# Entry of the expert loop: where the second norm's sums, the slot lists and the routing of a mixture-of-experts layer are worked out

## The reference, cut to what matters

```python
x = x + g1 * (merged @ w_out[l])                                # output projection of the mixers
h = rmsnorm(x, norm_ffn_g[l]) * (1.0 + sc2) + sh2               # second norm
y = swiglu(h2, w_shared_gu[l], w_shared_down[l]) + moe_routed(h2, router_w[l], router_bias[l], w_exp_gu[l], w_exp_down[l])
x = x + g2 * y
# moe_routed: scores = sigmoid(h2 @ router_w); the 6 best of 64 experts by scores + bias;
#   gate = score / sum of the 6 scores * 2.5; every expert runs SwiGLU (1024 -> 256 -> 1024) on its tokens,
#   and each token adds its 6 results, each times its gate
```

## Time and profile before

| what | us |
|---|---|
| median of 3 runs (lowest, highest) | 3300.69 (3299.34, 3303.19) |
| the profiled execution, its own time | 3301.01 |
| its span, first to last instruction | 3299.4 |
| busy TensorE / VectorE / ScalarE / GpSimd | 2927.4 / 2033.5 / 1552.3 / 578.8 |
| mean granted clock of TensorE | 0.937 of full |
| DMA mean | 204 GB/s |

### The profile page before, as it was taken

One profiled execution on the slowest core, in us unless ns is written; L12 is line 12 of the kernel. 1 busy time (PEld: TensorE's weight loads), 2 busy tenths in 40 slices (PEclk: granted clock), 3 DMA queues, 4 the chain that ended last, 5 costly groups with the idle time before them and its releaser, 6 DMA issues. The chain is left out here.

```text
span 3299.4 us, 42492 instructions
## 1 busy us (share of the span) xinstructions
PE 2927.4 (89%) x13828; PEld 2230.6 (68%) x13828; DVE 2033.5 (62%) x2874; ACT 1552.3 (47%) x2406; POOL 578.8 (18%) x569
## 2 busy tenths in 40 slices
PE   2899998899879999999369999989997999999983
PEld 1577776677667777777256777756775777777762
DVE  3544446555568888888345444464546788888854
ACT  0342333432347777777023324243223677777740
POOL 0100000000143333333010000000003333333310
PEclk9899999999889999999669999999987999999985
DMA  8123332224369999997422243312334899999944
GB/s 206 60 90 114 122 121 97 80 103 139 121 255 362 369 369 368 357 364 294 159 64 71 95 141 108 128 58 91 130 126 170 301 369 352 371 366 366 360 149 178
DMA packets 119235, 671.95 MB, mean 204 GB/s; under 512 B 27372, under 2 KB 28652, under 8 KB 84364
## 3 DMA queue, kind: packets, MB, share of 16 engines
q1 hardware_dynamic: 86476, 608.19, 50.2%
q0 software_dynamic: 31456, 57.70, 5.3%
q10 hardware_dynamic: 1152, 4.19, 0.3%
HBM read 655.20 MB, written 56.98 MB: 216 GB/s over the span
## 5 line engine op out<-in xcount | busy, mean ns | idle before, releaser
L1790 DVE TENSOR_TENSOR ew_lo<-ew,e_hi 128x2048 fp32r<-128x2048 f32 x256 | 586.7, 2292 | 187.4 <-ACT e_hi L1649 187.3
L670 PE MATMUL bank<-h_hi,w_hi 128*128 128x512 f32 x1248 | 515.0, 413 | 39.2 <-DVE gt L753 14.3
L1649 ACT ACTIVATE e_hi<-ew 128x2048 fp32r<-128x2048 f32 x256 | 489.8, 1914 | 102.1 <-PE bank L1935 78.3
L604 DVE TENSOR_TENSOR w_lo<-raw,w_hi 128x1024 fp32r<-128x1024 f32 x198 | 242.7, 1226 | 426.7 <-ACT w_hi L596 426.5
L670 PE MATMUL bank<-h_hi,w_lo 128*128 128x512 f32 x1248 | 503.7, 404 | 0.0
L670 PE MATMUL bank<-h_lo,w_hi 128*128 128x512 f32 x1248 | 501.3, 402 | 0.0
L1935 PE MATMUL bank<-e_hi,x_hi 128*128 128x512 f32 x1024 | 413.2, 404 | 0.0
L1935 PE MATMUL bank<-ew_lo,x_hi 128*128 128x512 f32 x1024 | 402.3, 393 | 0.0
L1935 PE MATMUL bank<-e_hi,x_lo 128*128 128x512 f32 x1024 | 400.1, 391 | 0.0
L1558 POOL DMA_INDIRECT y_d<-y,idx x128 | 217.4, 1698 | 623.8 <-issue 526.3
L596 ACT ACTIVATE w_hi<-raw 128x1024 fp32r<-128x1024 f32 x198 | 208.3, 1052 | 250.4 <-DMA raw<-in_wmix 179.2
(11 more groups left out here) (293 smaller groups left out, 4474.3 us busy)
## 6 DMA issues: line engine op xcount, KB each, us to landing
ew<-in_wexp SPq DMA_DIRECT2D x128, 2048.0 KB, 9.6
raw<-in_wmix SPq DMA_DIRECT2D x294, 512.0 KB, 4.0
ew<-in_wexp SPq DMA_DIRECT2D x128, 1024.0 KB, 9.3
yt<-y_d SPq DMA_DIRECT2D x8, 3072.0 KB, 10.1
ada<-in_ada SPq DMA_DIRECT2D x4, 2048.0 KB, 18.0
ew<-in_wexp SPq DMA_DIRECT2D x2, 3072.0 KB, 10.4
h_d<-htok ACTq DMA_DIRECT2D x8, 512.0 KB, 2.9
v_d<-vB SPq DMA_DIRECT2D x1, 3840.0 KB
```

The source lines that it names most:

```text
L604: nc.vector.tensor_tensor(w_lo[q % SPLIT][:], raw[u % RAW][:], w_hi[q % SPLIT][:].bitcast(F32), ALU.subtract).then_inc(lo_done, 1)
L670: ins = nc.tensor.matmul(out, lhs, rhs, start=start, stop=stop)
L1649: nc.scalar.activation(e_hi[h][:], up_part(ew, j, h), ACT.Copy).then_inc(whi_done, 1)
L1790: nc.vector.tensor_tensor(up_part(ew_lo, j, h), up_part(ew, j, h), e_hi[h][:].bitcast(F32), ALU.subtract).then_inc(wlo_done, 1)
```

## The change: what it does

- **Norm sums.** They leave the block of the experts. Beside the output projection ScalarE squares block k of `xT` one job after it was made, and TensorE adds one matmul of 512 columns with a column of ones (float32, result 1 x 512). The new block starts with a copy of that row to `srow`, four matmuls that turn it into a column for each token block, the mean, the root and the spread as before.
- **Norm's application.** VectorE does all 8 `hf` first; ScalarE adds all 8 shifts, loads the sigmoid's table by an early dummy, makes 3 of the `h_hi`, the sigmoid, and the others between the copies to `htok`. The logits wait for `hf` only.
- **Routing beside the shared expert.** TensorE runs jobs 0 and 1 before the ranks and 2 and 3 behind them, then the slot lists, jobs 4 to 9, the turning of expert 0's tokens, jobs 10 and 11. VectorE's routing is laced with the splits and evacuations of those jobs.
- **Slot lists.** VectorE makes `at_slot` (a pair's rank against 0 to 127, 24 x 128 values a partition); GpSimd makes `filed` (one-hot times result row + 1, and one-hot times gate: two instructions of 1536 values a partition); 24 matmuls of 128 columns sum their products into a bank (slot x expert): result row + 1 and gate. VectorE makes `slots` from it, and the gathers start from there. The write to `slot_d` remains (overflow blocks read it), 3 indirect DMAs in each of the first 8 steps of GpSimd's loop. The filling of `xg` with zeros and the reading back are gone.
- **Result rows.** Row choice*512 + token instead of token*6 + choice; the last block's load therefore reads 6 pieces of 4 KB, 2 MB apart, for a token.
- **Early first split.** ScalarE and VectorE split the weights of expert 0 while TensorE works on the down projection of the shared expert (`e_hi` and its neighbours now lie where `h_hi` and `h_lo` were, free after job 3). The list of overflow blocks moves behind expert 0's gate and up. SyncE's queue loads the weights of experts 1 and 2 only when `dest` and the slot lists are there.

```diff
@@ -1330,7 +1341,11 @@ (ScalarE, mixers)
-                    act_stream(act, events_of(whole(jobs["out"])))
+                    for m, j in enumerate(jobs["out"]):
+                        act_stream(act, events_of(whole([j])))
+                        if m:
+                            square_out(act, m - 1)
+                    square_out(act, KD - 1)
@@ -1422,11 +1437,23 @@ (TensorE, mixers)
+                    def sum_out(k):
+                        if k == 0:
+                            wait_mb_free(pe, ("st", "x2"))
+                        pe.wait_ge(xs_ready, k + 1)
+                        nc.tensor.matmul(MB[0:1, :], ones[:, 0:1], sn[k % 2][:], start=k == 0,
+                                         stop=k == KD - 1).then_inc(xs_used, 1)
+                    for m, j in enumerate(jobs["out"]):
                         pe_products(pe, j, 0, n_products(j))
+                        if m:
+                            sum_out(m - 1)
+                    sum_out(KD - 1)
@@ -1471,9 +1498,10 @@ (SyncE)
+                    sp.wait_ge(dest_ready, 1)
+                    sp.wait_ge(slots_full, 1)
                     load_up(1, 1)
                     load_down(1, 1)
-                    sp.wait_ge(dest_ready, 1)
@@ -1616,12 +1653,19 @@ (ScalarE, experts)
-                    norm_squares(act, "x2", xT)
                     split_hi(act, MIX_TILES)
-                    act_norm_apply(act, "x2", mod[:, 24:32], h_hi, [hf[:, k, :] for k in range(KD)])
...
+                    high(0, 3)
+                    act.wait_ge(logits_ready, 1)
+                    nc.scalar.activation(sgt[0:NE, :], OB[0:NE, :], ACT.Sigmoid).then_inc(score_ready, 1)
+                    high(3, 4)
+                    rows(0)
+                    high(4, 6)
+                    rows(1)
+                    high(6, KD)
+                    rows(2)
+                    rows(3)
                     act_stream(act, events_of(whole(jobs["shared"])), NTILES)
@@ -1682,7 +1737,7 @@
-                    act.wait_ge(mark, shared_mark)
+                    act.wait_ge(mark, up_mark)
                     w_half(0, 0, 0, 0)
@@ -1712,12 +1767,48 @@ (VectorE, experts)
-                    norm_squares(dve, "x2", xT)
-                    dve_norm_mean(dve, "x2")
+                    dve.wait_ge(xs_used, KD)
+                    nc.vector.tensor_copy(srow[0:1, :], MB[0:1, :]).then_inc(xr_ready, 1)
...
                     split_lo(dve, MIX_TILES)
+                    wait_mb_full(dve, ("rb", "x2"))
+                    for k in range(KD):
+                        nc.vector.scalar_tensor_tensor(hf[:, k, :], xT[:, k, :], amul[:, k:k + 1], MB[:], ALU.mult,
+                                                       ALU.mult).then_inc(nt_ready, 1)
...
+                    low(4, KD)
+                    weights_low(0)
                     link(dve, nc.vector.tensor_copy(topf[:], topi[:]))
...
+                    dve.sem_inc(sel_ready, 1)
+                    weights_low(1)
...
+                    for t in range(TC):
+                        pairs = slice(t * TOPK, (t + 1) * TOPK)
+                        nc.vector.tensor_tensor(at_slot[:, pairs, :], iota[:].unsqueeze(1).broadcast_to([P, TOPK, BLK]),
+                                                destf[:, pairs].unsqueeze(2).broadcast_to([P, TOPK, BLK]), ALU.is_equal
+                                                ).then_inc(at_slot_ready, 1)
+                    weights_low(3)
+                    job_out(3)
...
+                    weights_low(4)
+
+                    dve.wait_ge(slots_full, 1)
...
+                    nc.vector.tensor_scalar(slots[:, :, 0], slots[:, :, 1], SKIP | (S - 1), None, ALU.bitwise_and
+                                            ).then_inc(slots_set, 1)
...
+                    for i in range(4, 12):
+                        job_out(i)
+                        if i in (5, 8):
+                            first_weights(i // 8)
+                        if i == 10:
+                            x_half(0, 0)
                     w_half(0, 0, 1)
@@ -1878,6 +2013,11 @@ (TensorE, experts)
+                    shared_job(0)
+                    shared_job(1)
                     pe.wait_ge(sel_ready, 1)
...
-                    for j in jobs["shared"]:
-                        pe_products(pe, j, 0, n_products(j))
+                    shared_job(2)
+                    shared_job(3)
+                    pe.wait_ge(filed_ready, 2)
+                    for i in range(NPAIR):
...
+                        ins = nc.tensor.matmul(OB[:, 0:2 * NE], at_slot[:, i, :], filed[:, i, :, :].rearrange("p a e -> p (a e)"),
+                                               start=i == 0, stop=i == NPAIR - 1)
+                    ins.then_inc(slots_full, 1)
...
+                    for i in range(4, 10):
+                        shared_job(i)
...
                     transposes(0, 0, 0)
-                    for j in range(4):
+                    shared_job(10)
+                    shared_job(11)
+                    step(0, 0, first=True)
+                    list_blocks()
@@ -2004,7 +2158,7 @@
-            y_rows = y_d.rearrange("(t k) d -> t k d", k=TOPK)
+            y_rows = y_d.rearrange("(k t) d -> t k d", k=TOPK)
```

229 lines of the change are left out of this document (153 added, 76 removed).

## The result

The changed kernel takes 3304.8 us (median of 20 runs, 3298.0 to 3314.7), the kernel before on the same chip 3298.0 (20 runs): ratio 1.0020, 95% interval 1.0011 to 1.0029. It is a little slower there (0.2%), where 3275.5 was forecast. The profiled execution spans 3300.6 us at a mean granted clock of 0.943 (before 3299.4, 0.937). So a gain of 25 us was forecast; by the medians 6.8 us were lost, by the two spans 1.2.

What follows compares the result with a forecast made beforehand. TensorE was taken as the bound, fully busy in the expert loop, so only an earlier loop start gains: 14.6 - 2 = 12.6 us a layer, 25.2 in all, 3301.0 to 3275.8, forecast 3275.5; eight in ten 3262 to 3290.

Steps and rivals of the forecast that it cites:

- 1, norm sums: Start of the expert block: 13 us of sums removed, nothing won; first hf 0.6 us later, bound by tile 0's load.
- 2, logits: Entry of the expert block: logits take 8.8 us and end at 876.2, before 878.2.
- 3, shared expert first: Entry: the shared expert's job 0 starts at 885.3 instead of 892.50; the ranks come later and take 3.2 us.
- 4, slot lists: Entry: matmuls for the lists take 5.7 us, `filed` 1.8 to 7.2 and hidden; `slots` at 920.4.
- 5, first gather: Entry's end: gather issued 921.5, not 941.17, landing in 9.0; TensorE waits 3.2; loop starts 14.6 us earlier a layer.
- 6, "GpSimd and queues in the loop": First 8 loop steps: three writes with gather and scatter fill 7.0 of 9.7 us; weight loads still arrive; loss zero.
- 7, result rows: Between loop and next layer: loads in 4 KB pieces take 8.1 us each, +2 a layer, bounds 0 and +4.
- Rival C: Result-row loads between loop and next layer slow the kernel; at twice the time, 14.2 us each, 3329 us; chance 0.06.
- silu distances above 9.8 in the first 8 experts: Expert loop: sign that the forecast is wrong, DMA or GpSimd starving the loop; 9.70 was expected from the second on.
- B: Entry cold or starved: up to 8 us a layer, half of it likely, 3284 us, with all 3292; chance 0.20.

Runs made afterwards that it cites:

- r3: Changed kernel with eleven slot_d writes parked in GpSimd's wait for the first y, and three tile loads issued at the mixers' block's end; 3296.7 us, ratio 1.0002.
- r2: Changed kernel with all 24 slot_d writes issued ahead of the first gather and none in the loop; 3319.7 us, ratio 1.0076 to the kernel before.
- r5: Changed kernel with 18 slot_d writes moved into the hardware loop, three in eight steps, and three tile loads issued earlier; 3263.5 us, ratio 0.9817.
- the spread run: Another name for r5, the changed kernel with 18 slot_d writes spread over the hardware loop; 3263.5 us, and 3264.3 on a second chip.

## Why the prediction was wrong, step by step

**1, norm sums: right in its claim, one size off.** Each sum beside a job cost 1.18 us (jobs 6.62 apart instead of 5.44), not 0.9, and six of them, not seven, lie ahead of the last addition: it is 7.0 and 7.3 us later, measured from merged (6 x 1.18 = 7.1), not 6.3. The two slips partly cancel. From the block's start at 864.95 to the first `hf` it is 9.71; the step had 9.6, with tile 0 as the bound, and r3 shows that bound by lifting it. Tile 0's load was issued 2.4 behind the block's start and landed 5.0 later (4.7 taken).

**2, logits: +1.** The logits took 9.63 for 16 passes instead of 8.8; their end is 21.0 us behind the block's start instead of 19.9.

**3, shared expert first: right.** Job 0 starts 29.5 behind the block's start (29.0 predicted), the rank matmuls 42.4 (42.4), and they take 2.9 (3.2).

**4, slot lists: right.** Matmuls 5.52 (5.7), `filed` 2.77 and 3.46, inside 1.8 to 7.2 and hidden. `slots` is complete 63.2 us behind the block's start (64.1).

**5, first gather: right.** It landed in 9.4 (9.0), TensorE waited 2.99 (3.2), the overflow list took 0.24 (0.2). Block start to silu 0 is 86.4, predicted 85.4; the entry gained 13.6 and 18.0 us, predicted 14.6. Against the second profile of the kernel before (161.6 and 162.0) it gained 15.3 and 16.4.

**6, "GpSimd and queues in the loop": here it failed.** The step put the loop's loss at zero; it was 14.4 and 8.4 us in the two layers. The term "three writes (3.8)" in "3.8 + 2.2 + 1.0 = 7.0 of a 9.7 step" was sized by the earlier trace rows, writes made in the quiet entry. In the loop such an instruction takes 1.6 to 2.4 us in the mean of a run. And it isn't the only term that was too small: the other two, 2.2 for gather and scatter and 1.0 for what lies between, make 3.2, where the rows of before give 5.3. The kernel before had the evidence in the same view: its scatters took 1698 ns and its gathers 1474 in the loop, 991 and 1036 in the overflow block,

```profile
L1558 POOL DMA_INDIRECT y_d<-y,idx x128 | 217.4, 1698 | 623.8 <-issue 526.3 <-DVE y L1446 97.5
L1533 POOL DMA_INDIRECT xg<-h_d,idx x128 | 188.6, 1474 | 217.3 <-issue 203.5 <-POOL idx L1528 13.8
L1608 POOL DMA_INDIRECT y_d<-y,idx x2 | 2.0, 991 | 43.2 <-DVE y L1849 43.2
```

and each gather carries about 1.6 us of "issue" (203.5 / 128). Summed by these rows a step is 1.7 + 0.3 + 1.5 + 1.6 + 0.2 = 5.3. With three writes by the earlier trace rows (1.06 + 0.3 each) that is 9.4 of 9.70, a step with no room; with three of 1.6 + 0.3, their size in the changed kernel, it is 11.0, against the 11.3 measured. So of the 4.3 us that the step is longer than its 7.0, about half lies in the writes and half in the gather and scatter and their issue. What made the two halves dear is by the rows the same: an indirect DMA that starts inside a split of VectorE lasts until that split has ended and 0.8 to 0.9 us more, and of the changed kernel's 130 gathers 108 start so, of its 130 scatters 111. Step 5 took VectorE for the one that waits beside GpSimd; here it is GpSimd. The step over 9.70, less the head start, is the loss that the table has. SyncE's weights, the other part of step 6, cost nothing that the runs can show: r2 and r5 keep their later issue and have loops of 600 to 603.

**The drain: a step that wasn't there.** 8.25 us a layer (16.5 in all) appeared at a block's end that I had put at nothing, because no engine's work was changed there. I can't say that it was to be had from the trace of before: that shows 1.12 for the expert block and 3.32 for the mixers' block, a difference that nobody had asked about.

**7, result rows: +2 was wrong, 0 is right.** It took 10.0 and 17.2 us to landing against 10.1 and 17.1. Packets under 8 KB rose from 84364 to 90412 and the time did not. Rival C falls with it. The rule of the Trainium skill that stands beside C (DMA: Bandwidth & Descriptors, Latency and other measured facts) is for a pitch from one partition to the next, and here that pitch is 4 KB; no run tests it, and its 19 us a load did not come.

**The rivals.** None of the four had GpSimd as the engine that becomes the bound, though step 6 did its sum, and though the last paragraph names what came as a sign of being wrong (silu distances above 9.8 in the first 8 experts, "DMA or GpSimd starve the loop"): in layer 0 they were 10.8, 10.2 and 12.2 for experts 5 to 7, then 18.1 for expert 9. I had called GpSimd hidden with 2.7 us to spare, so its failure was given no chance of its own, and "slower" got 0.05. B's 3284 to 3292 was nearest to the 3304.8, and for another reason. A claim "7.0 of 9.7" with a term whose size was taken from another place in the program should have been a rival.

## What to carry to other kernels

Cost an instruction by the row of its like in the stretch where it will run, not by its own row in the stretch that it leaves: the same indirect DMA took 1.02 us on GpSimd in the entry and 1.6 to 2.4 in the loop. Look at what runs beside it: here its length went by the VectorE instruction that it started in. When an engine has a head start of a few steps, ask for its sum in a step against the bound's. A step over by 1.6 us was paid back late and mostly in one or two stalls (4 to 14 us each over the runs), not step by step, and spreading the same work one to a step removed them. And look at the drains of the blocks' ends: they are on nobody's busy time and still on the path.

## What the runs showed that I had not expected

- GpSimd's `slot_d` writes: 0.97 or 0.98 us at the least in every kernel, 1.02 to 1.06 on average where all 24 lie in the entry, 1.6 in steps 0 to 7, 2.16 to 2.37 in the hardware loop, single ones up to 4.11. Those that don't start inside one of VectorE's splits take 0.98 to 1.01 in the changed kernel, the others end 0.85 to 0.90 behind the split. No run took the splits away to try it.
- GpSimd's drain at a block's end takes 0.082 us for each DMA that it has issued since some point: 40 in 3.32 us, 114 in 9.37, 115 in 9.45, 118 in 9.70, 122 in 10.02; beside the 9.37 no DMA queue moved a packet. Where that point lies was settled only for writes in unrolled steps.
- Loads of 3 MB whose six pieces of 4 KB a partition lie 2 MB apart land as fast as contiguous ones (10.0 and 17.2 us against 10.1 and 17.1).
- The kernel before takes 3297 to 3299 us on some chips and 3322 to 3324 on others, while the changed kernel (3304.8, 3304.5) and the spread run (3263.5, 3264.3) take the same on one of either sort. I have no profile of the kernel before on one of the second sort; the cause is open.
